# First mixer of a two-block transformer kernel: modulation sums behind the probability copies, token mixing in other PSUM banks, output block begun between the joins, last output block summed by token tile

## The reference

```python
m = silu(c) @ mod_w[l] + mod_b[l]            # six modulation vectors of 1024 per layer
h = rms_norm(x, norm1_g) * (1 + sc1) + sh1
q, k, v, ua, va = split(h @ w_in)
attn  = window_attention(rope(q), rope(k), v, k_ctx, v_ctx, sink)     # 8 heads of 64
mixed = einsum('gpq,bcqgd->bcpgd', w_s, norm(gelu(va))) + b_s         # 8 groups of 64
y = concat([attn, gelu(ua) * mixed]) @ w_out
x = x + g1 * y
h2 = rms_norm(x, norm2_g) * (1 + sc2) + sh2
x = x + g2 * peer_ffn(h2, ...)               # 128 rows of a table of experts per token
```

## Time and profile before

| | |
|---|---|
| median of 3 runs | 2701.79 us (2700.58 to 2706.22) |
| the profiled execution | 2701.16 us, of which the profile's span 2699.2 us |
| PE busy | 2379.7 us, 88% |
| DVE busy | 1850.7 us, 69% |
| ACT busy | 1218.4 us, 45% |
| first mixer, from its first probability transposes to the barrier | 116.5 to 188.5 us |
| gathers of expert rows | 219 to about 1550 us |

### The profile page before, as it was taken

One profiled execution on the slowest core, in us unless ns is written; L12 is line 12 of the kernel. 1 busy time (PEld: TensorE's weight loads), 2 busy tenths in 40 slices (PEclk: granted clock), 3 DMA queues, 4 the chain that ended last, 5 costly groups with the idle time before them and its releaser, 6 DMA issues. The chain is left out here.

```text
span 2699.2 us, 35251 instructions
## 1 busy us (share of the span) xinstructions
PE 2379.7 (88%) x12931; PEld 1581.0 (59%) x12932; DVE 1850.7 (69%) x3444; ACT 1218.4 (45%) x2588; POOL 650.3 (24%) x547
## 2 busy tenths in 40 slices
PE   6988788888889888888788889999999998978999
PEld 4774333333335444343333268898888887856887
DVE  4767866677667867777765566676666666796665
ACT  4433434444444544444434454456445444445543
POOL 0003445554444444455544400000000000003000
PEclk8988999999999999999999999999999998978999
DMA  9689999999999999999999955542555554312553
GB/s 390 254 340 413 403 427 427 427 425 425 425 412 417 379 426 408 427 427 427 427 423 427 427 178 187 186 160 95 178 186 181 187 186 166 104 50 111 181 186 116
DMA packets 121705, 811.26 MB, mean 301 GB/s; under 512 B 15713, under 2 KB 18825, under 8 KB 26584
## 3 DMA queue, kind: packets, MB, share of 16 engines
q0 software_dynamic: 74160, 540.05, 47.9%
q1 hardware_dynamic: 47400, 269.32, 27.8%
HBM read 807.12 MB, written 1.15 MB: 299 GB/s over the span
## 5 line engine op out<-in xcount | busy, mean ns | idle before, releaser
L1411 PE MATMUL bank<-rows,diag 128*128 128x512 f32 (+1 forms) x2060 | 994.6, 620 | 213.2 <-ACT diag L1568 212.6
L1806 DVE CUSTOM_DVE_ANT_0 rows<-rows,h 128x1024 f32<-128x1024 f32 (+1 forms) x512 | 620.1, 1224 | 359.9 <-DMA rows<-in_peer_rows,idx 353.3
L1411 PEld LDWEIGHTS bank<-rows,diag 128*128 128x128 f32 (+1 forms) x2060 | 372.2, 194 | 738.8 <-ACT diag L1568 417.4
L1290 POOL DMA_INDIRECT rows<-in_peer_rows,idx x512 | 614.9, 1201 | 736.0 <-PE bank L1411 672.0
L1559 ACT ACTIVATE picks<-picks 128x1 f32<-128x1 f32 (+1 forms) x512 | 103.3, 202 | 635.7 <-DVE picks L1806 614.8
L2151 PE MATMUL bank<-hT_pair,halves 128*128 128x512 f32 x864 | 307.4, 399 | 0.5 <-DVE hT_pair L2029 0.4
L2152 PE MATMUL bank<-hT_pair,halves 128*128 128x256 f32 x864 | 242.2, 280 | 0.0
L1568 ACT ACTIVATE diag<-const_table,picks 128x128 f32<-128x128 f32 (+1 forms) x512 | 205.5, 401 | 48.0 <-ACT picks L1563 1.1
L2085 DVE TENSOR_TENSOR halves<-weight_ring,halves 128x2048 fp32r<-128x2048 f32 x74 | 169.3, 2288 | 74.5 <-ACT halves L2080 74.3
L2151 PEld LDWEIGHTS bank<-hT_pair,halves 128*128 128x128 f32 x864 | 162.3, 188 | 41.4 <-DVE hT_pair L2029 0.9
L1323 PE MATMUL bank<-halves_b,halves_a 128*128 128x256 f32 x912 | 172.1, 332 | 0.0
(11 more groups left out here) (573 smaller groups left out, 3773.1 us busy)
## 6 DMA issues: line engine op xcount, KB each, us to landing
weight_ring<-in_ffn_w_gate SPq DMA_DIRECT2D x44, 1024.0 KB, 4.9
weight_ring<-in_ffn_w_up SPq DMA_DIRECT2D x44, 1024.0 KB, 4.9
weight_ring<-in_ffn_w_down SPq DMA_DIRECT2D x44, 1024.0 KB, 4.8
mod_ring<-in_mod_w SPq DMA_DIRECT2D x16, 1024.0 KB, 7.6
weight_ring<-in_peer_w_q SPq DMA_DIRECT2D x16, 1024.0 KB, 9.3
half_ring<-in_mod_w SPq DMA_DIRECT2D x24, 512.0 KB, 7.5
rows<-in_mod_w SPq DMA_DIRECT2D x12, 1024.0 KB, 7.8
weight_ring<-in_attn_w_in SPq DMA_DIRECT2D x12, 1024.0 KB, 4.8
```

Of the source, the lines that this page charges most:

```text
L1290: nc.gpsimd.indirect_dma_start(ring[:, s], None, dram["peer_rows"], bass.IndirectOffsetOnAxis(ap=idx[:, T, n:n + 1], axis=0)).then_inc(row ...
L1411: mm = nc.tensor.matmul(bank[:, :], diag[0:n, j % DIAG_SLOTS], ring[0:n, j % ROW_SLOTS, D + half * 512:D + (half + 1) * 512], start=(j in ...
L1806: dotted.up(nc.vector.tensor_tensor_reduce(out=ring[r, s, 0:D], in0=ring[r, s, 0:D], in1=its_h, scale=1.0, scalar=0.0, op0=ALU.mult, op1=A ...
```

## The change

1. On DVE, the three `rows.accumulate` that stood behind probability copies 1, 3 and 5 now stand together behind all eight copies.
2. `mix_tokens` writes PSUM banks 2 and 3, not 0 and 1, and `join` reads them there.
3. On DVE, `make_low` of the first output block stands ahead of `scale(1)`, and `rows.add` stands behind both joins instead of ahead of them.
4. On PE, output product 0 is made in two pieces: its first 12 matmuls (T = 0, first four k) stand behind `turn_cat(1)`, ahead of `turn_cat(2)` and `turn_cat(3)`; the other 36 follow these and two `rows.multiply` that stood behind product 0.
5. The last output product puts T = 0 and T = 1 into two banks, and DVE gates and adds each tile when it is done (four operations of 128x256 for two of 128x512), with the next stage's `make_low` between the two. The 128x1024 operation on `vec[:, 0]` moves from ahead of the last add to behind the third.
6. ACT takes the square sum and root of token tile 0 at the end of the first block, beside the last product, and no longer in `experts`.

```diff
@@ first_block, tensor
-                        for k in range(KD):
-                            ready(T, k)
...
+                def last_product(b):
...
+                        if T == 0:
+                            half_done.up(mm)
+                    mm.then_inc(W.multiplied, 1)
@@
-                        mm = nc.tensor.matmul(kit.bank[g // 4][:, g % 4 * P:(g % 4 + 1) * P], ws[g // 4][:, g % 4, :],
+                        mm = nc.tensor.matmul(kit.bank[2 + g // 4][:, g % 4 * P:(g % 4 + 1) * P], ws[g // 4][:, g % 4, :],
@@
-                mix_tokens()
-                turn_cat(1)
-                turn_cat(2)
-                turn_cat(3)
...
-                for j in range(no):
+                mix_tokens()
+                turn_cat(1)
+                wait_copied(2 * HEADS - 1)
+                product(nb, bank(0), ready=ready, steps=every[:4])
+                turn_cat(2)
+                turn_cat(3)
+                rows.multiply(pe, 2)
+                product(nb, bank(0), ready=ready, steps=every[4:]).then_inc(W.multiplied, 1)
+                for j in range(1, no):
                     if j >= 2:
                         pe.wait_ge(projected.sem, pr0 + j - 1)
-                    product(nb + j, bank(j), ready=ready if j == 0 else at_once).then_inc(W.multiplied, 1)
-                    if j < 2:
+                    if j == no - 1:
+                        last_product(nb + j)
+                        continue
+                    product(nb + j, bank(j)).then_inc(W.multiplied, 1)
+                    if j == 1:
                         rows.multiply(pe, 2)
@@ first_block, scalar
+                act.wait_ge(projected.sem, pr0 + no + 1)
+                kit.act(nc.scalar.activation(mixed_sums, x[:, 0], ACT.Square, accum_out=first_root[:, 0:1]))
+                squares.up(nc.scalar.activation(first_root[:, 1:2], first_root[:, 0:1], ACT.Sqrt, scale=1.0 / D, bias=kit.eps))
@@ first_block, vector
+                def add_last():
+                    cols = slice((no - 1) * BLK, no * BLK)
+                    for T in range(NT):
+                        if T == 0:
+                            dve.wait_ge(half_done.sem, 1)
+                        else:
+                            dve.wait_ge(W.multiplied, b0 + nb + no)
+                        projected.up(nc.vector.tensor_tensor(tmp[:, T], last_of(T), g1[:, cols], ALU.mult))
+                        dve.wait_ge(projected.sem, pr0 + no + 2 * T)
+                        projected.up(nc.vector.tensor_tensor(x[:, T, cols], x[:, T, cols], tmp[:, T], ALU.add))
+                        if T == 0:
+                            make_low(nb + no)
@@
-                    if j in (1, 3, 5):
-                        rows.accumulate(dve, 1)
                     if j == 2:
                         rows.add_sum(dve, 1)
+                rows.accumulate(dve, 3)
@@
+                make_low(nb)
                 scale(1)
-                rows.add(dve, 4)
-                make_low(nb)
                 join(0)
                 join(1)
+                rows.add(dve, 4)
@@ experts, vector
-                inverse(T, T + 1)
+                if T == 0:
+                    dve.wait_ge(squares.sem, s0 + 1)
+                    kit.dve(nc.vector.reciprocal(ss[:, 2, 0:1], first_root[:, 1:2]))
+                else:
+                    inverse(1, 2)
```

More of the change, by code:

```diff
@@ L574, in opening, with first_block @@
     W.used += nb
-def first_block(kit, dram, rows, vec, bias, shared):
+def first_block(kit, dram, rows, vec, bias, shared, first_root):
     nc, W, x = kit.nc, kit.weights, kit.x
@@ L599, in first_block @@
         flat = lambda a: a[:].rearrange("p k n -> p (k n)")
+        mixed_sums = flat(kit.hT)[:, D:2 * D]
         spare, late, mixed_in = flat(hcT), vec[:, 2:4].rearrange("p a n -> p (a n)"), flat(kit.h)
@@ L626, in first_block @@
         gi0 = gate_in.n
+        squares, half_done = kit.count("squares_summed"), kit.count("last_block_half_done")
+        last_of = lambda T: (bank(no - 1)[:, 0, :], kit.bank[4][:, 0:BLK])[T]
         with nc.Block() as block:
@@ L685, in at_once @@
                     pass
-                def product(b, out, between={}, ready=at_once):
+                every = [(T, k) for T in range(NT) for k in range(KD)]
+                def last_product(b):
                     pe.wait_ge(split.sem, p0 + b + 1)
@@ L690, in product @@
                     for T in range(NT):
+                        if T:
+                            pe.wait_ge(cat_low.sem, cl0 + 1)
                         for k in range(KD):
-                            ready(T, k)
                             for n, (w, t) in enumerate([(lo, x_hi), (hi, x_lo), (hi, x_hi)]):
[L694 to L698, removed]
+                                mm = nc.tensor.matmul(last_of(T), t[:, k, T * P:(T + 1) * P], w[:, k, :],
+                                                      start=(k == 0 and n == 0), stop=(k == KD - 1 and n == 2))
+                        if T == 0:
+                            half_done.up(mm)
+                    mm.then_inc(W.multiplied, 1)
+                def product(b, out, between={}, ready=at_once, steps=every):
+                    pe.wait_ge(split.sem, p0 + b + 1)
+                    hi, lo = (a[b % 2].rearrange("p (k n) -> p k n", k=KD) for a in (w_hi, w_lo))
+                    for T, k in steps:
+                        ready(T, k)
+                        for n, (w, t) in enumerate([(lo, x_hi), (hi, x_lo), (hi, x_hi)]):
+                            mm = nc.tensor.matmul(out[:, T, :], t[:, k, T * P:(T + 1) * P], w[:, k, :],
+                                                  start=(k == 0 and n == 0), stop=(k == KD - 1 and n == 2), skip_group_check=True)
+                        if (T, k) in between:
+                            score(between[T, k])
+                            score(between[T, k] + 1)
                     return mm
@@ L1074, in _ @@
                         rows.accumulate(dve, 1)
[L1075 to L1078, removed]
+                    if j == no - 1:
+                        add_last()
+                        continue
                     add_gated(j)
@@ L1082, in _, with experts @@
                         rows.add_sum(dve, 2)
-                    if j + 2 < no + 1:
+                        dve.wait_ge(loaded.sem, l0 + 16 * 8)
+                        kit.dve(nc.vector.scalar_tensor_tensor(out=vec[:, 0], in0=vec[:, 1], scalar=1.0, in1=vec[:, 0],
+                                                               op0=ALU.add, op1=ALU.mult))
+                    else:
                         make_low(nb + j + 2)
         W.used += nb + no
-def experts(kit, dram, rows, vec, late_bias, shared):
+def experts(kit, dram, rows, vec, late_bias, shared, first_root):
     nc, W = kit.nc, kit.weights
@@ L1158, in experts @@
     l0, s0, n0, t0, hi0, lo0, hm0, sp0 = (c.n for c in (loaded, squares, normed, turned, high, low, high_made, split))
-    hm0, sp0 = hm0 - 1, sp0 - 1
+    hm0, sp0, s0 = hm0 - 1, sp0 - 1, s0 - 1
     q0, e0, sc0, c0, to0, sh0, ex0, ch0, ga0, d0, w0, su0, k0 = (c.n for c in (
@@ L1537, in take_turned @@
                     high.up(nc.scalar.copy(place(x_hi, T, k), spread(j)))
-            for T in range(NT):
-                kit.act(nc.scalar.activation(junk, x[:, T], ACT.Square, accum_out=ss[:, 0, T:T + 1]))
-                squares.up(nc.scalar.activation(ss[:, 1, T:T + 1], ss[:, 0, T:T + 1], ACT.Sqrt, scale=1.0 / D, bias=kit.eps))
+            kit.act(nc.scalar.activation(junk, x[:, 1], ACT.Square, accum_out=ss[:, 0, 1:2]))
+            root(1, 2)
             for j, (T, k) in enumerate(jobs):
@@ L3914, in build @@
         shared = (halves_a, halves_b)
-        with kit.sb("vectors", [P, 4, D]) as vec:
+        with kit.sb("vectors", [P, 4, D]) as vec, kit.sb("first_root", [P, 2]) as first_root:
             with kit.sb("c_wide", [P, KD, 32]) as cwide:
@@ L3923, in build @@
                     first_block(kit, dram, rows, vec, [(early[0:P:32, :, :], early[:], bias[:, 0:4]),
-                                                       (line[0:P:32, :, :], line[:], bias[:, 4:7])], shared)
-                experts(kit, dram, rows, vec, bias[:, 7:10], shared)
+                                                       (line[0:P:32, :, :], line[:], bias[:, 4:7])], shared, first_root)
+                experts(kit, dram, rows, vec, bias[:, 7:10], shared, first_root)
         second_block_start(kit, dram, shared)
```

2 lines of the change are left out of this document (1 added, 1 removed).

## The result

The changed kernel took 2715.13 us (median of 5 runs, 2714.05 to 2717.99) beside 2702.68 us for the kernel before (5 runs, 2700.58 to 2706.22): ratio 1.0047, 95% interval 1.0036 to 1.0058, so 0.5% slower. Forecast were 2690.4 us and a faster kernel. The profiled execution is that of 2715.13 us.

The account below looks back on a forecast made before the run. Transfers bind the late gathers, PE and DVE waits the mixer ahead; 6.7 + 1.5 + 3.1 = 11.3, less 0.5, gives 10.8 us, so 2701.16 - 10.8 = 2690.4 us. Likeliest range 2687.5 to 2693, wider 2686 to 2696.5.

Parts of the forecast that it names:

- What the gathers see: Late chunks and gathers: the full stretch of transfers begins 10.8 us sooner, at the same rate; 2690.4 us.
- (c): Output products: PE stays at 1.2 GHz, four products lose 19 us, the kernel is slower at 2709 us; chance 0.03.
- signs of being wrong: Mixer: PE waiting at 150 to 162 us, the clock falling in the products, or late chunks and first gather moving separately.
- limit of some 358 GB/s on loads: Mixer loads, 124 to 192 us: at this rate 20.0 MB need 55.9 us where 53.4 are free; 2693 us.
- Accumulations: Mixer, DVE's accumulations behind all copies: PE is past the chunk at 124.9 instead of 131.6 us, 6.7 us sooner.
- Joins: Mixer, other banks and low half first: joins done at 147.6 instead of 155.75 us, 1.5 us beyond the loop's shift.
- Two pieces: Output product 0 split: from the joins to product 1 takes 7.2 us instead of 10.3, so 3.1 us gained.
- 0.5 us of waiting: Output products: PE waits this long for the two chunks behind product 1, between 0 and 3 us.
- rival (a): Mixer: the loads bind, chunks behind product 1 land 3 to 5 us late; 3 to 6 us more, chance 0.12.
- cover for the loads: Mixer: the loads fit into the shortened time before the full stretch of transfers, by 0.4 to 3 us.
- 10.8 us: Late chunks: issued this much sooner, at 180.6 us, from 6.7 + 1.5 + 3.1 = 11.3, less 0.5.
- Last product and root: End of the first block, last product by tile and earlier root: 2.1 us for the engines, nothing for the transfers.

Follow-up runs that it names:

- e3: Kernel before with 32 unused bytes ahead of the row ring only, the first block's modulation rings unmoved; 2723.12 us, ratio 1.0076.
- e1: Changed kernel with first_root in unused bytes behind eps, so every tile stands where it stood before the change; 2692.65 us, ratio 0.9965.
- e9: Kernel before with only the three accumulations moved behind all eight probability copies, tiles unmoved; 2694.76 us, ratio 0.9969.
- e5: Changed kernel with first_root in unused bytes and the two chunks behind product 1 moved behind product 2; 2689.06 us, ratio 0.9949.
- e2: Kernel before with an unused 32 bytes behind vectors, moving the modulation rings and the row ring; 2723.9 us, ratio 1.0079.
- e4: Kernel before with an unused 64 bytes behind vectors, moving mod_ring, half_ring and the row ring; 2720.72 us, ratio 1.0063.
- e6: Kernel before with 32 unused bytes behind the row ring, moving only the experts' small tiles; 2702.73 us, ratio 0.9999.
- e7: Kernel before with 128 unused bytes ahead of the row ring, which then begins at 150144; 2718.87 us, ratio 1.0059.
- e8: Kernel before with the 768-byte tile places allocated ahead of the row ring, which then begins at 150784; 2703.73 us, ratio 1.0002.

## Why the prediction was wrong

**The step that failed** is under "What the gathers see": "The full stretch of transfers shifts", and its DMA share afterwards would be 1.01 "at the same rate". The stretch did shift, by 4.9 us at the first gather. It did not keep its rate: 420 GB/s instead of 427, since the tile `first_root`, which the changed code reads and writes, moved the row ring by 32 bytes. That is 17.0 us between the first and the last gather, and 20.7 us for a whole run in e3. The profiled spans, 2713.3 and 2699.2 us, add up: 4.9 us less to the first gather, 17.0 more in the gathers, 2.0 more behind the start of the last. The prediction counted instructions, waits and bytes, and took a tile of 8 bytes to cost nothing. Of the rivals none was this one: (c) had the right sign and a wrong cause, as no product ran at 1.2 GHz as a whole. Two of the prediction's own signs of being wrong came as well, PE's wait for a chunk (from 161.6 us) and a clock of 0.89 from 164 to 184 us, but they cost about 4 us and not the 25 between forecast and time. The limit of some 358 GB/s on loads that the prediction took from the Trainium skill, "DMA: Bandwidth & Descriptors", section "Where 436 GB/s comes from", does not show in the changed kernel: it moved 394 GB/s from 132 to 164 us.

**With the tile put elsewhere the sum nearly held.** e1 measured 2692.65 us against 2690.4, inside the range. Its late chunks went at 182.78 and not at 180.6 us, and the wait for chunks behind product 1 came out at 0.6 us here and at 3.2 in the changed kernel; that the sum held this well is partly luck. Term by term:

- *Accumulations*, 6.7 us to the token mixing: 6.9 in the changed kernel (120.22 to 144.55 is 24.3 us, 118.98 to 150.18 was 31.2), 6.7 in e9. Right.
- *Joins*: forecast from 145.4 to 147.6 us, measured 146.35 to 148.50 in an execution that was 1.2 us late. Right. The wait of 3.18 us is gone, as said.
- *Two pieces*, 3.1 us: the new sum of 7.2 us was right (7.3), but the 3.1 us were booked on the wrong edit. 1.3 belong to the pieces.
- *0.5 us of waiting* for the chunks behind product 1, "between 0 and 3": mis-sized. 3.2 us in the changed kernel, and behind them the second chunk at 1.79 us and product 2 in 6.7 us (167.59 to 174.31) instead of 5.95, so 4.7 in all (19.07 us from product 1 to the last product, 14.33 before); 0.6 in e1. The bytes were counted, but not what PE loses at the low clock behind such a wait, and the loads landed up to 14.3 us after their issue. This is a part of rival (a), which priced it at 3 to 6 us. The prediction's cover for the loads, 0.4 to 3 us, is 0.8 to 3.6 when its quotients are not rounded (20.0 MB at 380 and 402 GB/s), which changes no choice.
- *10.8 us* for the late chunks: 5.6 in the changed kernel, 8.6 in e1, 12.3 in e5. In the changed kernel the loop began 1.24 us late and the waits cost 4.2 more than the 0.5 allowed, together about the 5.2 us that are missing. Profiled executions differ here by themselves: with the mixer of before unchanged, the late chunks go at 191.1 to 194.5 us in e2, e3, e4, e6, e7 and e8. Nor did the 32 bytes under `mod_ring` and `half_ring` visibly make the loop late: it began at 119.2, 119.5 and 120.2 us in the three kernels that moved them (e2, e4, the changed one) and at 118.4 to 121.5 us in the ten others. Whether they had a part in the later loads is open; e2 less e3 is 0.8 us, with intervals of 3.8 us to either side.
- *Last product and root*, 2.1 us for the engines: mis-sized. DVE's first reciprocal of the norm stood 3.7 us behind PE's end (190.05 and 186.35) and stands 2.2 behind it now (183.03 and 180.82), so 1.5 us. DVE ends 1.2 us behind PE, not 0.9, and then waits 1.05 us, not 0.6. That the transfers gain nothing by it was right: in the seven traces read for this, the late chunks go 4.9 to 5.2 us behind PE's end with or without these edits.

## What to carry to other kernels

When a change allocates anything, list where every later tile begins, before and after. A ring that takes transfers at the full rate should begin at a multiple of 256 bytes; 32 bytes more ahead of it cost 21 us here, twice what all the scheduling in this change gave. Where a stage without any changed instruction gets slower at an unchanged DMA share, compare GB/s at that share before looking for a wait, and try a pure shift of addresses on the old kernel: it takes one line and settles it.

## What the runs showed of the hardware

- The place of a transfer's destination inside the partition changes its rate: 427 GB/s at multiples of 256 bytes (two places), 420 or 421 at remainders of 32, 64 and 128 (from 1100 to 1150 us), some 4.4 ns for a packet. The small tiles behind the ring, moved by 32 bytes, cost nothing that can be told (e6, 0.9999, interval 0.9989 to 1.0008).
- A load takes longer from issue to landing where more is on its way: 4.8 to 8.2 us for chunks in the kernel before, where 346 GB/s were moving from 132 to 164 us, and up to 14.3 us in the changed one, where it was 394. That the queue ahead of it is the reason is our reading; no run changed it alone. The same row of the changed kernel:

```profile
DMA to landing us min/median/max: 5.2/7.9/14.3
```

- A wait of PE of 3.2 us in two parts was followed by 1.6 us of longer matmuls, 0.8 in the two chunks and 0.8 in the product (4.7 us in all, less the waits). In e5, where the wait is gone, so are they.
